# Norm sums of block 1 as two one-pass products of split squares, in a two-block transformer kernel on one core

## The chip, the core and the metric

The kernel runs on one core of a Trainium2 chip. The core has a matrix engine (TensorE, PE in the rows), a vector engine (VectorE, DVE), an activation engine (ScalarE, ACT), GpSimd (POOL) and a queue engine that issues the transfers (SP). Each takes its instructions in the order in which the program lists them and waits at an instruction until its semaphores have the value it asks for. The metric is the device time of one execution, in microseconds (us), the median of several. The engines share SBUF; products are written to PSUM, which has eight banks of 128 x 512 numbers.

## The reference

One sequence of 512 tokens, width 1024, float32. Block 1 (a parallel mixer: attention and a gated delta rule, both from one projection of the normed input) is what is changed; block 2 (stick-breaking attention, differential attention, two feed-forward layers) follows and is untouched. What matters of block 1:

```
q = apply_rope(rms_norm(heads(aq), q_norm)); k = apply_rope(rms_norm(heads(ak), k_norm))   # 8 and 2 heads
o_att = gqa_attention(q, k, v)
y_att = (o_att * silu(az)) @ w_br_att
qkv = silu(short_conv(concat([dq, dk, dv])))
qd = l2_norm(heads(cq)) * DN_DK ** -0.5 ; kd = l2_norm(heads(ck))                          # 8 and 8 heads
o_dn = bidir_gated_deltanet(qd, kd, vd, g, beta)
o_dn = rms_norm(o_dn, dn_norm)                                                             # 8 heads
y_dn = (o_dn * silu(dz)) @ w_br_dn
mix = (sigmoid(gate_att) * y_att + sigmoid(gate_dn) * y_dn) @ w_out
```

Both norms need, for each token, the sum of 128 squares of a head: 10 times for attention, 16 times for the convolved q and k, 8 times for the output.

## The kernel before

Everything is held feature-major: a tile is 128 features by 512 tokens. A sum over the features of a head is a product with a 128 x 128 matrix of ones, which also spreads the sum over all partitions.

**Projections.** Weights stream from memory in pairs of 1 MB, are split into a rounded high part (ACT, `w_hi`) and a rest (DVE, `w_lo`, line 2286), both in the type float32r, and each 128 x 128 block of weights gives three one-pass products of 512 columns (high by high, high by low, low by high). The high and low parts of the input lie in `hh` and `hl`, those of the weights in `spl`. Eight blocks, 24 products, make one output tile (a "projection"). They go to PSUM banks 0 and 1 in turn.

**Lanes.** All the rest of block 1 runs between these products. For each of 8 heads there are lanes: `rope_lane` (norm and rotation of attention's q), `att_lane`, `conv_lane` (five taps, SiLU, norm, for q, k and v), `prep_lane` (decay products, then a triangular inverse in levels of 32 x 32 products, `lv_m`, `lv_x`, ending in the 64 x 64 products `lv_q1` and `lv_q2`), `scan_lane` (four steps of `sc_r`, `sc_v`, `sc_s`, `sc_o`) and `out_lane` (the output norm: `on_a` squares it, `on_b` sums and applies it). A head's scan can begin once its `lv_q2` is through.

**The order** is set before the program runs, by `arrange`: it walks through the projections and keeps one clock per engine, adding a given cost for each step (0.86 us for a sum over features, `PE_B`; 0.69 for a DVE operation, 0.62 for an ACT operation). A lane's next step is put between two products when the lane's time and the engines it names are not ahead of PE's clock. Where the projections need something of a lane (`o.until`), the lane's steps are put down one after the other, with no product between them, until it is there. Such places are: a free pad before a convolution's projection; a free slot for the gated `dz` before its projection (`dz_slots`: the slot of head hd is given back by `on_b` of head hd - 2); a free bank; and, for the products of `w_br_att` (`ya`), each of its eight operands. These operands are reloaded from memory after `lv_q2` of head 7, split by ACT (`re_hi`) and DVE (`re_lo`, line 2529), and `ya` waits for the k-th before its k-th block.

**The sums** that are changed are plain float32 products: `ar_ss` (attention, its square in an `arena` tile), `cv_r` (convolution, its square in a `pad` or `x` tile), `on_b` (its square in `on_t`). In the rows a product is named by its output, its moving and its stationary operand: `ps<-pad,cst` is a square times the ones in `cst`; one plain product is two records there. In the scan `arena` alone (128x128) and `rv,arena` are `sc_v`, `rv,kdt` is `sc_s`, `arena,rv` is `sc_o`, `st,arena` is `sc_r`, `arena,st` the part of the state, `sc_oq`; in attention `x,arena` is the output (`at_o`), `cst,x` a transpose, `arena` with 512 columns the scores.

Of the kernel before, what the change touches and what calls it, by code (L numbers as in the profile page):

```python
# [234 lines left out]
def arrange(o, n_pairs):  # L235
# [161 lines left out]
    def rope_in(key, u):  # L397
# [4 lines left out]
        st = o.add("ar_in", key, cost=[("AC", AC_B), ("AC", AC_B)], after=u.t)  # L402
# [6 lines left out]
    def rope_lane(key, u):  # L409
# [136 lines left out]
    keep, work, acc, pads = Slots(2), Slots(1), Slots(2), Slots(4)  # L546
# [73 lines left out]
    def conv_lane(i, ip, t_in):  # L620
# [35 lines left out]
        st = o.add("cv_sq", i, cost=[("AC", AC_B)])  # L656
        st.ia, st.ip = ia, ip
# [7 lines left out]
        st = banked("cv_r", i, cost=[("PE", PE_B), ("AC", AC_B), ("AC", AC_B)])  # L665
        st.ip = ip
# [122 lines left out]
    def out_lane(hd, ikeep, ou):  # L789
        keep.give(ikeep, scan_last[hd])  # L790
        yield "AC"
        st = o.add("on_a", hd, cost=[("AC", AC_B), ("AC", AC_B)])
        st.u = ou
        obank.give(ou)
        yield "PE"
# [3 lines left out]
        st = banked("on_b", hd, cost=[("PE", PE_B), ("AC", AC_B), ("AC", AC_B), ("DV", DV_B), ("DV", DV_B)])  # L799
# [709 lines left out]
def build(nc, wstream, wba, consts, vecs, cossin, pos, xT, pT, outT):  # L1509
# [6 lines left out]
    with ctx:  # L1516
        def sb(name, shape, dt=F32):
            return ctx.enter_context(nc.sbuf_tensor(name, shape, dt))
# [39 lines left out]
        const_r = sb("const_r", [128, 320], F32R)  # L1558
        CR = {"neg_tri_l": const_r[:, 0:128]}
# [270 lines left out]
        def tensor(pe):  # L1830
# [9 lines left out]
            for q in steps:  # L1840
# [52 lines left out]
                elif kind == "ar_ss":  # L1893
# [3 lines left out]
                    w.wait_ge(*ar_in_done(q.key[0]))  # L1897
                    mm(psum[u.b][:, :], C["ones"], tmp_of.get(q.key[0], ar_tmp)[2], True, True).then_inc(filled[u.b], 1)
# [68 lines left out]
                elif kind == "cv_r":  # L1967
# [3 lines left out]
                    w.wait_ge(sem("cv_sq"), at["cv_sq", q.key[0]].n)  # L1971
                    mm(psum[u.b][:, :], C["ones"], pad_of[q.ip], True, True).then_inc(filled[u.b], 1)
# [149 lines left out]
                elif kind == "on_b":  # L2122
# [653 lines left out]
        def scalar(act):  # L2776
# [57 lines left out]
            for q in steps:  # L2834
# [589 lines left out]
```

## Time and profile before

| | us |
|---|---|
| runs | 2187.49, 2189.46, 2189.53; median 2189.46 |
| span of the profiled execution | 2186.7 |
| median over this span | 2.8 |
| busy in the span: PE, DVE, ACT, POOL | 2133.8, 1247.0, 1038.3, 224.2 |
| heads of block 1, 60 to 720 us: PE, DVE, ACT busy | 637.1, 424.5, 396.0 of 660 |

The profile gives one execution; its span is from its first to its last instruction, and the 2.8 us above it are the difference to the median of the timed runs. "Busy" of PE is the time in which some product is under way. Products overlap, so what one costs in a row of products is the step from its start to the start of the next, not its duration.

### The profile page before, as it was taken

How to read it: one execution, taken by the hardware profiler on the slowest of the kernel's cores; microseconds unless marked ns; L12 is line 12 of the kernel's file. 1: busy time of each engine (PE TensorE's matmuls, PEld its weight loads, DVE VectorE, ACT ScalarE, POOL GpSimd, SP SyncE). 2: the span in 40 equal slices, each digit the busy share in tenths (PEclk: the TensorE clock that was granted, in tenths of full speed). 3: DMA queues.
4: the chain of work that ended last, by engine and by line, in shares of the span. 5: the costliest groups of instructions: out<-in, count | busy, mean ns of one | idle time of the engine just before them, and what ended most of it. 6: DMA issues, size and time to landing. Idle time of an engine off the chain costs nothing.

```text
span 2186.7 us, 35850 instructions
## 1 busy us (share of the span) xinstructions
PE 2133.8 (98%) x14982; PEld 1685.9 (77%) x14982; DVE 1247.0 (57%) x2247; ACT 1038.3 (47%) x2012; POOL 224.2 (10%) x240
## 2 busy tenths in 40 slices
PE   8999999999999999999999999999999999999999
PEld 6777676777777887877777888888777777888887
DVE  6667677666654456655557542445577676443442
ACT  6656565566555235656655332233455544332331
POOL 0112221221220010100001000000101001000000
PEclk9999999999999999999999999999999999999999
DMA  4221211221214432211112222222211112222222
GB/s 177 99 79 63 78 65 50 89 68 50 97 50 153 142 135 78 70 67 59 58 39 82 97 97 97 97 97 97 82 62 63 63 59 97 97 97 96 97 97 77
DMA packets 36226, 186.68 MB, mean 85 GB/s; under 512 B 4560, under 2 KB 4944, under 8 KB 16992
## 3 DMA queue, kind: packets, MB, share of 16 engines
q1 hardware_dynamic: 36064, 184.38, 24.7%
q8 instruction: 118, 1.93, 0.4%
q14 instruction: 44, 0.36, 0.1%
HBM read 172.80 MB, written 7.90 MB: 83 GB/s over the span
## 4 chain that ended last, share of the span: by engine, by line
PE 89%; DVE 6%; ACT 3%; issue 2%; DMA 0%; SPq 0%; POOL 0%; DVEq 0%; ACTq 0%
PE ps L1834 88%; PE ps L1837 1%; ACT arena L2779 1%; DVE spl L2286 1%; ACT spl L2782 0%; ACT hh L2779 0%; DVE x L2644 0%; DMA raw<-wstream 0%; DVE x L2402 0%; DVE arena L2587 0%; DVE x L2573 0%; DVE arena L2485 0%; DVE arena L2569 0%; DVE hl L2595 0%; ACT on_t L2779 0%
## 5 line engine op out<-in xcount | busy, mean ns | idle before, releaser
L1834 PE MATMUL ps<-hh,spl 128*128 128x512 f32 (+1 forms) x3152 | 1024.1, 399 | 6.4 <-DVE hl L2577 2.1
L1834 PEld LDWEIGHTS ps<-hh,spl 128*128 128x128 f32 x3152 | 584.6, 189 | 139.5 <-issue 19.6
L1834 PE MATMUL ps<-hl,spl 128*128 128x512 f32 (+1 forms) x1568 | 620.8, 396 | 0.0
L2286 DVE TENSOR_TENSOR spl<-raw,spl 128x512 fp32r<-128x512 f32 x596 | 421.2, 731 | 153.6 <-ACT spl L2782 152.4
L1834 PE MATMUL ps<-arena_r,spl 128*128 128x512 f32 x1968 | 467.2, 392 | 10.3 <-DVE arena_r L2298 8.4
L1834 PEld LDWEIGHTS ps<-arena_r,spl 128*128 128x128 f32 x1968 | 371.1, 189 | 89.6 <-issue 10.5
L2782 ACT ACTIVATE spl<-raw 128x512 fp32r<-128x512 f32 x596 | 345.3, 619 | 143.9 <-PE ps L1834 138.8
L1834 PEld LDWEIGHTS ps<-hl,spl 128*128 128x128 f32 x1568 | 295.9, 189 | 63.0 <-issue 9.1
L1834 PE MATMUL ps<-arena 32*32 32x32 f32 (+6 forms) x5664 | 218.2, 224 | 16.8 <-issue 10.5
L2779 ACT ACTIVATE arena<-arena 128x512 f32<-128x512 f32 (+3 forms) x220 | 142.3, 648 | 189.7 <-DVE arena L2649 140.8
L1834 PEld LDWEIGHTS ps<-arena 32*32 32x32 f32 (+4 forms) x5664 | 126.2, 116 | 98.2 <-issue 79.4
L2782 ACT ACTIVATE arena_r<-arena 128x512 fp32r<-128x512 f32 x64 | 40.3, 631 | 197.0 <-DVE arena L2656 191.7
L2644 DVE TENSOR_TENSOR x<-x,ps 128x512 f32<-128x512 f32 x64 | 43.8, 684 | 133.6 <-PE ps L1834 133.6
L2779 ACT ACTIVATE arena<-ps 128x256 f32<-128x256 f32 (+5 forms) x116 | 69.0, 599 | 99.8 <-PE ps L1834 98.2
L2779 ACT ACTIVATE arena<-ps,small 128x512 f32<-128x512 f32 (+3 forms) x126 | 70.9, 566 | 90.0 <-DVE small L2745 53.9
L3248 POOL TENSOR_TENSOR arena<-arena 128x512 f32<-128x512 f32 x29 | 38.6, 1332 | 616.0 <-ACT arena L2779 616.0
L1834 PE MATMUL ps<-spl,hh 128*128 128x256 f32 x512 | 98.0, 291 | 2.7 <-DVE pad L2720 1.5
L2653 DVE TENSOR_TENSOR arena<-ps,arena 128x512 f32<-128x512 f32 x44 | 30.4, 691 | 104.4 <-PE ps L1834 104.4
L1834 PEld LDWEIGHTS ps<-spl,hh 128*128 128x128 f32 x512 | 80.8, 192 | 9.9 <-issue 6.2
L2649 DVE TENSOR_TENSOR arena<-ps,arena 128x512 f32<-128x512 f32 x44 | 30.4, 691 | 77.2 <-PE ps L1834 74.8
L1834 PE MATMUL ps<-spl,hl 128*128 128x256 f32 x256 | 72.6, 284 | 0.0
L2782 ACT ACTIVATE arena<-ps 128x256 f32<-128x256 f32 (+2 forms) x88 | 39.5, 449 | 65.0 <-PE ps L1834 51.2
(258 smaller groups left out, 2117.0 us busy)
## 6 DMA issues: line engine op xcount, KB each, us to landing
raw<-wstream SPq DMA_DIRECT2D x148, 1024.0 KB, 4.9
arena<-spill SPq DMA_DIRECT2D x17, 256.0 KB, 5.3
GS<-g_rows SPq DMA_DIRECT2D x16, 256.0 KB, 3.4
spill<-x SPq DMA_DIRECT2D x14, 256.0 KB, 2.0
arena<-arena SPq DMA_DIRECT2D x18, 128.0 KB, 2.2
x<-xT SPq DMA_DIRECT2D x4, 512.0 KB, 6.4
spill<-arena SPq DMA_DIRECT2D x8, 256.0 KB, 2.0
x<-xT SPq DMA_DIRECT2D x1, 2048.0 KB, 7.8
```

The costliest lines, as they stand in the source:

```text
L1834: return pe.matmul(out, lhsT, rhs, start=start, stop=stop, skip_group_check=True)
L1837: return pe.transpose(out, in_, C["ident"])
L2286: tt(spl[:, p % 2, 1, c], raw[:, p % 2, c], spl[:, p % 2, 0, c].bitcast(F32), ALU.subtract) \
L2644: tt(X[q.m], X[q.m], psum[q.u.b][:, :], ALU.add).then_inc(drained[q.u.b], 1)
L2649: tt(f_sl[q.i], psum[q.u.b][:, :], SQ[q.name][2], ALU.mult).then_inc(drained[q.u.b], 1)
L2653: tt(p, psum[q.u.b][:, :], SQ[q.g.name][2], ALU.mult).then_inc(drained[q.u.b], 1)
L2779: return act.activation(out, in_, func, **kw)
L2782: return act.activation(out, in_, ACT.Copy)
L3248: tt(acc, acc, tmp[q.i], ALU.add).then_inc(sem("sq_pool"), 1)
```

## The change

Each of the 34 sums becomes two one-pass products, of the high part of the square and of its rest, with ones in float32r (`ones_r`). For this, ACT writes the square a second time, rounded to float32r, and DVE subtracts the two (`ar_lo`, `cv_lo`, `on_lo`). Five tiles are added to the arena, the high part of the convolution has two slots (`sq_hi`), and the gates' semaphores are merged into one. The costs given to `arrange` change with it: 0.46 for a sum (`PE_S2`), an operation more on ACT and on DVE. Since `arrange` decides by these costs, the whole order of block 1 is another one. The last line of the diff makes room in SBUF.

```diff
+PE_S2 = 0.46
@@ rope_in, rope_lane
-        st = o.add("ar_in", key, cost=[("AC", AC_B), ("AC", AC_B)], after=u.t)
+        st = o.add("ar_in", key, cost=[("AC", AC_B)] * 3, after=u.t)
...
+        yield "DV"
+        o.add("ar_lo", key, cost=[("DV", DV_B)])
         yield "PE"
         while not ring.ready():
             yield "PE"
-        banked("ar_ss", key, cost=[("PE", PE_B), ("AC", AC_B), ("AC", AC_B)])
+        banked("ar_ss", key, cost=[("PE", PE_S2), ("AC", AC_B), ("AC", AC_B)])
@@ conv_lane
-        st = o.add("cv_sq", i, cost=[("AC", AC_B)])
-        st.ia, st.ip = ia, ip
+        while not sq_hi.ready():
+            yield "AC"
+        ih, h_old = sq_hi.take()
+        o.behind(h_old)
+        st = o.add("cv_sq", i, cost=[("AC", AC_B), ("AC", AC_B)])
+        st.ia, st.ip, st.ih, st.h_old = ia, ip, ih, h_old
+        yield "DV"
+        st = o.add("cv_lo", i, cost=[("DV", DV_B)])
+        st.ip, st.ih = ip, ih
...
-        st = banked("cv_r", i, cost=[("PE", PE_B), ("AC", AC_B), ("AC", AC_B)])
+        st = banked("cv_r", i, cost=[("PE", PE_S2), ("AC", AC_B), ("AC", AC_B)])
@@ out_lane
-        st = o.add("on_a", hd, cost=[("AC", AC_B), ("AC", AC_B)])
+        st = o.add("on_a", hd, cost=[("AC", AC_B)] * 3)
         st.u = ou
         obank.give(ou)
+        yield "DV"
+        o.add("on_lo", hd, cost=[("DV", DV_B)])
@@ tensor: cv_r (ar_ss and on_b alike)
-                    w.wait_ge(sem("cv_sq"), at["cv_sq", q.key[0]].n)
-                    mm(psum[u.b][:, :], C["ones"], pad_of[q.ip], True, True).then_inc(filled[u.b], 1)
+                    w.wait_ge(sem("cv_lo"), at["cv_lo", q.key[0]].n)
+                    mm(psum[u.b][:, :], ones_r[:, :], cv_hi[q.ih], True, False)
+                    mm(psum[u.b][:, :], ones_r[:, :], pad_lo[q.ip], False, True).then_inc(filled[u.b], 1)
@@ vector
+                elif kind == "cv_lo":
+                    w.wait_ge(sem("cv_sq"), at["cv_sq", q.key[0]].n)
+                    tt(pad_lo[q.ip], pad_of[q.ip], cv_hi[q.ih].bitcast(F32), ALU.subtract).then_inc(sem("cv_lo"), 1)
@@ scalar: on_a
+                    f(on_hi, psum[q.u.b][:, :], ACT.Square)
                     f(on_e, psum[q.u.b][:, :], ACT.Square)
                     f(on_o, psum[q.u.b][:, :], ACT.Identity, scale=V("dn_norm")).then_inc(drained[q.u.b], 1)
@@
-    nc = _bacc.Bacc("TRN2", target_bir_lowering=False, num_devices=1)
+    nc = _bacc.Bacc("TRN2", target_bir_lowering=False, num_devices=1, dynamic_dma_scratch_size=1024)
```

**The first place that moves: PE, the scan of head 5.** Before, projection products (`hh,spl`, `hl,spl`) stand between its steps; from `lv_q2` (64x64) on:

```order
L1834 MATMUL ps<-arena 64x64 x8
L1834 MATMUL ps<-hl,spl 128x512
L1834 MATMUL ps<-x,arena 128x128 x4
L1837 MATMUL ps<-cst,x 128x128 x4
L1834 MATMUL ps<-arena 128x512
L1834 MATMUL ps<-arena 128x128 x2
L1834 MATMUL ps<-hh,spl 128x512 x2
L1834 MATMUL ps<-hl,spl 128x512
L1834 MATMUL ps<-hh,spl 128x512
L1834 MATMUL ps<-rv,kdt 128x128 x2
L1834 MATMUL ps<-arena,rv 128x128 x2
L1834 MATMUL ps<-hh,spl 128x512
```

Now it stands between the projections of head 6's `dz` and head 7's `dz`; from `lv_q2` (64x64) on:

```order
L1857 MATMUL ps<-arena 64x64 x8
L1857 MATMUL ps<-arena 128x128 x2
L1857 MATMUL ps<-rv,kdt 128x128 x2
L1857 MATMUL ps<-arena,rv 128x128 x2
L1857 MATMUL ps<-st,arena 128x128 x2
L1857 MATMUL ps<-rv,arena 128x128 x2
L1857 MATMUL ps<-arena,st 128x128 x2
L1857 MATMUL ps<-x,arena 128x128 x4
L1860 MATMUL ps<-cst,x 128x128 x4
L1857 MATMUL ps<-arena 128x512
L1857 MATMUL ps<-rv,kdt 128x128 x2
L1857 MATMUL ps<-arena,rv 128x128 x2
```

and it ends with `on_b`, the pair with `on_r`, before the first product of head 7's `dz`:

```order
L1857 MATMUL ps<-arena,rv 128x128 x2
L1857 MATMUL ps<-st,arena 128x128 x2
L1857 MATMUL ps<-rv,arena 128x128 x2
L1857 MATMUL ps<-arena,st 128x128 x2
L1857 MATMUL ps<-arena,rv 128x128 x2
L1857 MATMUL ps<-arena_r,ones_r 128x512
L1857 MATMUL ps<-on_r,ones_r 128x512
L1857 MATMUL ps<-hh,spl 128x512
L1857 MATMUL ps<-hl,spl 128x512
```

What moved: the 32 rows from `lv_q1` to `on_b` of this head hold no projection product, where before there were 48 between `lv_q1` and `on_b`. `on_b` of head 5 stands behind 1416 projection products, before behind 1269. Two shorter stretches of this sort are new as well: five half-levels of 32x32 products with one product of scores between them (behind product 1200), and two and two with one sum between them (behind 1512).

**The second place: PE and DVE at the end of head 7.** Before, its scan and `on_b` were over 42 products ahead of `ya` (the row of 576, whose moving operand is `arena_r`):

```order
L1834 MATMUL ps<-arena,rv 128x128 x2
L1834 MATMUL ps<-hh,spl 128x512
L1834 MATMUL ps<-hl,spl 128x512
L1834 MATMUL ps<-hh,spl 128x512 x2
L1834 MATMUL ps<-hl,spl 128x512
L1834 MATMUL ps<-hh,spl 128x512
L1834 MATMUL ps<-on_t,cst 128x512
L1834 MATMUL ps<-hh,spl 128x512
L1834 MATMUL ps<-hl,spl 128x512
L1834 MATMUL ps<-hh,spl 128x512 x2
L1834 MATMUL ps<-hl,spl 128x512
```

Now `ya` begins within the scan, and `on_b` stands between the blocks 3 and 4 of its first tile:

```order
L1857 MATMUL ps<-arena,rv 128x128 x2
L1857 MATMUL ps<-arena_r,spl 128x512 x2
L1857 MATMUL ps<-st,arena 128x128 x2
L1857 MATMUL ps<-arena_r,spl 128x512 x2
L1857 MATMUL ps<-rv,arena 128x128 x2
L1857 MATMUL ps<-arena,st 128x128 x2
L1857 MATMUL ps<-arena_r,spl 128x512 x2
L1857 MATMUL ps<-arena,rv 128x128 x2
L1857 MATMUL ps<-arena_r,spl 128x512 x3
L1857 MATMUL ps<-arena_r,ones_r 128x512
L1857 MATMUL ps<-on_r,ones_r 128x512
L1857 MATMUL ps<-arena_r,spl 128x512 x564
```

On DVE, `re_lo` of the eight operands (2529, now 2566) stood before like this around the two steps of `on_b` (2515 and 2518, now 2552 and 2555):

```order
L2529 TENSOR_TENSOR arena_r<-arena,arena_r 128x512
L2508 SCALAR_TENSOR_TENSOR st<-st,small,ps 128x128 x2
L2529 TENSOR_TENSOR arena_r<-arena,arena_r 128x512
L2495 SCALAR_TENSOR_TENSOR rv<-ps,small,arena 128x128 x2
L2529 TENSOR_TENSOR arena_r<-arena,arena_r 128x512 x2
L2515 TENSOR_TENSOR arena<-arena,on_t 128x512
L2518 TENSOR_TENSOR arena<-arena 128x512
L2286 TENSOR_TENSOR spl<-raw,spl 128x512
L2529 TENSOR_TENSOR arena_r<-arena,arena_r 128x512
```

and now:

```order
L2566 TENSOR_TENSOR arena_r<-arena,arena_r 128x512
L2545 SCALAR_TENSOR_TENSOR st<-st,small,ps 128x128 x2
L2532 SCALAR_TENSOR_TENSOR rv<-ps,small,arena 128x128 x2
L2566 TENSOR_TENSOR arena_r<-arena,arena_r 128x512 x2
L2313 TENSOR_TENSOR spl<-raw,spl 128x512
L2363 TENSOR_TENSOR on_r<-on_t,arena_r 128x512
L2552 TENSOR_TENSOR arena<-arena,on_t 128x512
L2555 TENSOR_TENSOR arena<-arena 128x512
L2566 TENSOR_TENSOR arena_r<-arena,arena_r 128x512 x3
L2313 TENSOR_TENSOR spl<-raw,spl 128x512
L2566 TENSOR_TENSOR arena_r<-arena,arena_r 128x512
```

What moved: `on_b` of head 7 stands behind 1692 projection products, before behind 1638; `ya` begins behind 1680 in both. The operands 4 to 6 of `ya` are split behind both steps of `on_b` on DVE, and PE asks for operand 4 right behind the sum of `on_b`.

## Rows read from the trace of the kernel before

**Rows 1.** Busy time by stretch: PE, PEld, DVE, ACT, POOL, clock, DMA share, GB/s.

```profile
60.00:720.00 660.00, 637.10 (x7820) 493.06 (x7819) 424.50 (x858) 396.03 (x795) 133.54 (x144) 0.99 0.23 79
```

**Rows 2.** PE's waits, 60 to 720 us: us in total, times, longest.

```profile
PE ps L1834 <- issue: 10.5, 11, 3.2
PE ps L1834 <- DVE arena L2485: 4.6, 7, 1.2
```

**Rows 3.** PE in order of time: start, us; a sum and its neighbours.

```profile
69.74 1.02 PE L1834 MATMUL ps<-pad,cst 128*128 128x512 f32 x2
...
70.83 0.40 PE L1834 MATMUL ps<-hl,spl 128*128 128x512 f32 x1
71.06 0.62 PE L1834 MATMUL ps<-hh,spl 128*128 128x512 f32 x2
```

**Rows 4.** Groups by line, 60 to 720 us: busy us, mean ns, idle before.

```profile
L2286 DVE TENSOR_TENSOR spl<-raw,spl 128x512 fp32r<-128x512 f32 x132 | 97.2, 751 | 28.2 <-ACT spl L2782 27.8
...
L2779 ACT ACTIVATE pad<-x 128x512 f32<-128x512 f32 x12 | 7.5, 627 | 5.0 <-DVE x L2407 3.8 <-DVE x L2402 1.3
```

**Rows 5.** PE in order of time: lv_q2 and on_b of heads 2, 3, 7.

```profile
315.71 0.68 PE L1834 MATMUL ps<-arena 64*64 64x64 f32 x16
...
342.04 1.02 PE L1834 MATMUL ps<-on_t,cst 128*128 128x512 f32 x2
...
380.39 0.68 PE L1834 MATMUL ps<-arena 64*64 64x64 f32 x16
...
403.48 1.10 PE L1834 MATMUL ps<-on_t,cst 128*128 128x512 f32 x2 [0.67 <-ACT arena L2779]
...
668.60 0.68 PE L1834 MATMUL ps<-arena 64*64 64x64 f32 x16
...
686.91 1.10 PE L1834 MATMUL ps<-on_t,cst 128*128 128x512 f32 x2
```

**Rows 6.** PE in order of time: pieces of attention, then of the scan.

```profile
516.93 1.05 PE L1834 MATMUL ps<-x,arena 128*128 128x128 f32 x8
517.82 0.60 PE L1837 MATMUL ps<-cst,x 128*128 128x128 f32 x4
518.26 1.02 PE L1834 MATMUL ps<-arena 128*128 128x512 f32 x2
...
671.72 0.67 PE L1834 MATMUL ps<-rv,kdt 128*128 128x128 f32 x4
...
672.59 0.48 PE L1834 MATMUL ps<-hl,spl 128*128 128x512 f32 x1
```

**Rows 7.** PE, ACT and DVE in order of time: two half-levels of head 7.

```profile
656.07 0.75 PE L1834 MATMUL ps<-arena 32*32 32x32 f32 x64
...
656.87 0.38 ACT L2782 ACTIVATE arena<-ps 128x256 f32<-128x256 f32 x1 [2.87 <-PE ps L1834]
...
659.41 0.42 DVE L2457 TENSOR_TENSOR arena<-arena,ps 128x256 f32<-128x256 f32 x1 [3.35 <-PE ps L1834]
659.87 0.45 DVE L2459 STREAM_TRANSPOSE arena<-arena 128x256 f32<-128x256 f32 x1
```

**Rows 8.** ACT and DVE in order of time: behind on_b of head 7.

```profile
688.04 0.69 ACT L2779 ACTIVATE on_t<-ps,small 128x512 f32<-128x512 f32 x1 [0.28 <-PE ps L1834]
...
689.43 0.69 DVE L2515 TENSOR_TENSOR arena<-arena,on_t 128x512 f32<-128x512 f32 x1 [3.40 <-ACT on_t L2779]
690.16 0.69 DVE L2518 TENSOR_TENSOR arena<-arena 128x512 f32<-128x512 f32 x1
```

**Rows 9.** PE in order of time, then stretches as in rows 1.

```profile
227.00 0.43 PE L1834 MATMUL ps<-arena 32*32 32x32 f32 x16 [3.22 <-issue]
...
222.00:224.00 2.00, 1.78 (x62) 1.18 (x53) 0.18 (x1) 0.90 (x2) 1.82 (x3) 1.00 0.95 383
...
225.00:230.00 5.00, 3.00 (x22) 2.12 (x21) 2.10 (x4) 0.60 (x1) 0.00 (x0) 0.64 0.01 3
230.00:235.00 5.00, 5.00 (x140) 3.92 (x140) 0.48 (x2) 2.10 (x5) 0.00 (x0) 0.68 0.00 0
```

More of the change, by code:

```diff
@@ L664, in conv_lane @@
             o.behind(o.at["pr_kk", hd - 1])
-        st = banked("cv_r", i, cost=[("PE", PE_B), ("AC", AC_B), ("AC", AC_B)])
-        st.ip = ip
+        st = banked("cv_r", i, cost=[("PE", PE_S2), ("AC", AC_B), ("AC", AC_B)])
+        st.ip, st.ih = ip, ih
+        sq_hi.give(ih, st)
         yield "DV"
@@ L798, in out_lane @@
         o.behind(o.at["dz_out", hd])
-        st = banked("on_b", hd, cost=[("PE", PE_B), ("AC", AC_B), ("AC", AC_B), ("DV", DV_B), ("DV", DV_B)])
+        st = banked("on_b", hd, cost=[("PE", PE_S2), ("AC", AC_B), ("AC", AC_B), ("DV", DV_B), ("DV", DV_B)])
         dz_slots.give(hd % 2, st)
@@ L1531, in build @@
         spl = sb("spl", [128, 2, 2, 2048], F32R)
-        x = sb("x", [128, KT, S])
+        with nc.sbuf_tensor("x", [128, KT, S], F32) as x:
+            pass
+        x_r = sb("x_r", [128, KT, S], F32R)
         hh = sb("hh", [128, KT, S], F32R)
         hl = sb("hl", [128, KT, S], F32R)
-        NA = 41
+        NA = 46
         with nc.sbuf_tensor("arena", [128, NA, S], F32) as arena:
@@ L1558, in build @@
         const_r = sb("const_r", [128, 320], F32R)
+        ones_r = sb("ones_r", [128, 128], F32R)
         CR = {"neg_tri_l": const_r[:, 0:128]}
@@ L1896, in tensor @@
                         w.wait_ge(drained[u.b], u.n - 1)
-                    w.wait_ge(*ar_in_done(q.key[0]))
-                    mm(psum[u.b][:, :], C["ones"], tmp_of.get(q.key[0], ar_tmp)[2], True, True).then_inc(filled[u.b], 1)
+                    w.wait_ge(sem("ar_lo"), at["ar_lo", q.key[0]].n)
+                    hi, lo = ar_halves(q.key[0])
+                    mm(psum[u.b][:, :], ones_r[:, :], hi, True, False)
+                    mm(psum[u.b][:, :], ones_r[:, :], lo, False, True).then_inc(filled[u.b], 1)
                 elif kind == "gate_mm":
@@ L2125, in tensor @@
                         w.wait_ge(drained[u.b], u.n - 1)
-                    t = at["on_a", hd].u
-                    w.wait_ge(drained[t.b], t.n)
-                    mm(psum[u.b][:, :], C["ones"], on_e, True, True).then_inc(filled[u.b], 1)
+                    w.wait_ge(sem("on_lo"), hd + 1)
+                    mm(psum[u.b][:, :], ones_r[:, :], on_hi, True, False)
+                    mm(psum[u.b][:, :], ones_r[:, :], on_lo, False, True).then_inc(filled[u.b], 1)
                 elif kind == "rstd" and q.last:
@@ L2275, in vector @@
             dve.tensor_copy(ident_r[:, :], C["ident"]).then_inc(sem("setup"), 1)
+            dve.tensor_copy(ones_r[:, :], C["ones"])
             dve.memset(eps, EPS).then_inc(sem("setup"), 1)
@@ L2881, in scalar @@
                     f(rs, k_in[i], ACT.Square)
+                    f(ar_halves(q.key[0])[0], k_in[i], ACT.Square)
                     f(t_, k_in[i], ACT.Identity, scale=V("k_norm")).then_inc(sem("ar_in"), 1)
@@ L2891, in scalar @@
                     f(rs, psum[q.u.b][:, :], ACT.Square)
+                    f(ar_halves(name)[0], psum[q.u.b][:, :], ACT.Square)
                     f(t_, psum[q.u.b][:, :], ACT.Identity, scale=qw).then_inc(drained[q.u.b], 1)
@@ L2898, in scalar @@
                     full(u)
-                    f(g3(beta), db, ACT.Exp, scale=-1.0).then_inc(sem("gate_eb"), 1)
+                    f(g3(beta), db, ACT.Exp, scale=-1.0).then_inc(sem("gate_act"), 1)
                     empty(u)
@@ L2948, in scalar @@
                     w.wait_ge(sem("cv_act"), at["cv_act", q.key[0]].n)
+                    if q.h_old:
+                        full(q.h_old.u)
+                    f(cv_hi[q.ih], acc_of[q.ia], ACT.Square)
                     f(pad_of[q.ip], acc_of[q.ia], ACT.Square).then_inc(sem("cv_sq"), 1)
```

31 lines of the change are left out of this document (21 added, 10 removed).

## The prediction

> **What bounds the kernel now.** I read the busy times first: over the heads of block 1, 60 to 720 us, PE is busy 637.1 of 660 us, DVE 424.5 (64%), ACT 396.0 (60%) [rows 1]. So PE is the bound, at close to full clock. Next come PE's waits: the largest is "issue", 10.5 us in 11 gaps, that is, gaps in which no semaphore was awaited; the second is the product behind `lv_q2`, 4.6 us in 7 [rows 2]. No wait on the ends of the norm sums is among the large ones. So a shorter product is time won as long as PE stays fed; what decides is whether the new order keeps it fed.
>
> **What is removed: three eighths of a sum each, on the path.** A plain sum starts at 69.74; the projection product behind the next one starts at 70.83, and the one after it 0.23 us later [rows 3]. So the sum and one projection product take 1.09 us, the sum alone 0.86. The pair is two one-pass products, 0.46 us. That is 0.40 us less for each of 34 sums: **-13.6 us**. The rows of a projection are the nearest ones for a pair, since they too change their weights at each product, so I give this term no more than 1 us either way.
>
> A page of the Trainium skill, "TensorE: Matmul & The Clock Gate" (section "Back-to-back issue gap"), gives a gap of N/2.4 ns plus 2.5 ns for one pass, 216 ns at 512 columns. By it the pair would be 0.43 us and the term -14.6 us. The row shows 0.23 us for one product in this kernel, and the row decides.
>
> **What is added on ACT and DVE, off the path.** 34 squares on ACT at 0.63 us, like the group with 128x512 in and out, and 34 subtractions on DVE at 0.75 us at most, like the one with the same shape and types [rows 4]: 21 and 26 us, by which ACT goes from 60% to 63% and DVE from 64% to 68%. Neither becomes the bound. In a chain that ends in a sum they come one behind the other and lengthen it by 0.6 + 0.7 = 1.3 us, which costs nothing while projection products stand between. They cost where none do.
>
> **What is moved: block 1's order.** The lanes come later against the projections: `on_b` of head 5 behind 1416 products, not 1269; of head 7 behind 1692, not 1638. Late lanes cost nothing by themselves. They cost at the places where the planner had to have something finished, and there put the steps of a chain one behind the other. Nothing of that sort stood in the order before. The places, one by one:
>
> *Head 5's scan, behind product 1416.* PE has to go through all rows from `lv_q1` to `on_b` before the next projection product. How long the chain takes is read from the same chain before: from `lv_q2` to `on_b` 26.3 us (head 2), 23.1 us (head 3), 18.3 us (head 7, with no attention beside it) [rows 5]. Part of the longer ones is the filling itself, so I take 22.3 us, add 1.3 us for the new square and subtraction, and 3 us from `lv_q1` to `lv_q2`, between which a piece of each kind of attention stands: 26.6 us. PE's own work in it: 17 pieces of the scan at 0.44 (7.4 us), four outputs of attention at 0.89, three transposes at 0.44 [rows 6], two scores at 0.86 like a sum, two 64x64 pieces at some 0.4 (an estimate), one pair: 15.3 us. Left over are 11 us; I book **+10**. The ends: with head 7's chain 7 us, with head 2's 15 us.
>
> *The levels, behind 1200 and 1512.* From a level's products to ACT 0.80 us, ACT 0.38; from the other half to DVE as long, and DVE 0.42 and 0.45 [rows 7]. So a half-level takes 1.2 and 1.7 us in turn, of which PE works 0.7. Five in a row with one product of scores: 5.9 - 4 x 0.7 - 0.86 = 2.2 us idle. Two pairs with a sum between: some 2 us. On top, such bursts run short of instructions: the ten "issue" gaps beside the largest come to 0.7 us each (10.5 less 3.2, over 10) [rows 2]; one or two more of them in nine dense bursts: 1 us. Together **+5**, ends 3 and 9. A further scan step without filling behind product 1104: **+1**.
>
> Here too a page speaks: "Runtime: NRT & Kernel Launch" of the Trainium skill, section "Instruction fetch mechanics", holds that fetching is hidden behind the pace of issue. This trace disagrees: PE stood still for 3.22 us within a burst, with nothing awaited, just as a load of weights moved 383 GB/s [rows 9]. By the page the places would be 1 us cheaper.
>
> *The end of head 7, behind 1680.* Now only 28 projection products are there to fill the scan and its `on_b`, not 34, and the chain is 1.3 us longer: 6 x 0.23 + 1.3 = 2.7 us. Then comes a new wait: PE asks for operand 4 of `ya` right behind the sum of `on_b`, and on DVE its `re_lo` stands behind both steps of `on_b`, which wait for ACT. Before, `on_b`'s sum began at 686.91 [rows 5], ACT took it up at 688.04, DVE at 689.43 and 690.16 [rows 8], so the split of operand 4 would end near 690.85 + 0.7 = 691.5. The pair begins at 687 and takes 0.46, so PE waits from 687.4 to 691.5: 4.1 us. Together **+7**, ends 4 and 9.
>
> **What goes with the old order.** The gap of 3.22 us, and what followed it: the granted clock was 0.64 and 0.68 in the 10 us from 225 to 235 us [rows 9], where half speed is 1.2 GHz; that is 3.4 us lost. A gap of this sort needs a burst just when weights land, and there are as many of both as before, so I count half of 6.6: **-3.3** (ends -6.6 and 0). Waits at head 5's old place, some **-1**.
>
> **The clock.** The new stretches have two idle times of 3 us and more: before `on_b` of head 5 (the last scan step, three ACT steps and the subtraction with nothing to fill), and before operand 4 of `ya`. Before the clock fell at 225 us, PE had idled for 3.22 us. One of the two will do it again: **+3.3**, ends 0 and 6.6.
>
> **The sum.** -13.6 + 10 + 5 + 1 + 7 - 3.3 - 1 + 3.3 = +8.4 us on a span of 2186.7: 2195.1. The median lies 2.8 us above that span: **2197.9 us**, against 2189.5.
>
> **The rivals.**
> 1. *The stretches are cheap* and the products' gain stays: all chains at their light end and no fall of the clock. -13.6 + 7 + 3 + 1 + 4 - 6.6 - 1 + 0 = -6.2 us, so 2183 us. For it: head 7's chain of 18.3 us shows what the scan needs without attention. Against it: attention is in the stretch of head 5, on the same ACT and DVE.
> 2. *They cancel.* Gain and new waits meet at 2185 to 2194 us, most simply when the clock doesn't fall and the luck of the old gap isn't repeated (8.4 - 3.3 - 3.3 = +1.8, so 2191 us).
> 3. *Instructions and clock.* The dense bursts run dry as at 223.8 us, and both idle times pull the clock down: 15 + 9 + 1 + 9 + 6.6 - 13.6 - 1 = +26 us, 2216 us. For it the gap of 3.22 us in a single burst, against it that the other ten gaps are short.
> 4. *The queues.* The added 21 and 26 us make ACT and DVE late in the dense stretches, so that ordinary steps arrive late at PE as well: 34 times 0.4 us is 14 us, which would eat the whole gain even if the stretches cost half: 2200 us. It decides from a DVE near 80%; the 64% of [rows 1] with the added work, 68%, speaks against it.
> 5. *The pair isn't cheaper*, if the new type slowed the plain products beside it: 0 instead of -13.6, 2211 us. Projection products of this type already stand beside plain ones [rows 3].
>
> **How the numbers follow.** The forecast (2194 to 2206 us) has 0.42; rival 1 0.19, rival 2 0.24, rival 3 0.06, rival 4 0.07, rival 5 0.02. A range of 8 in 10 has to take in rivals 2 and 4 and most of 1: 2182 to 2209 us. A measurement of this kernel can tell some 0.2% from no change, 4.4 us: faster is under 2185.1, slower over 2193.8. Faster 0.20, same 0.24, slower 0.56.
>
> **What would show it.** Right: PE's busy time down by some 14 us of products, `ps<-..,ones_r` at a step of 0.23 us; PE idle by some 10 us within the 27 us before `on_b` of head 5; a wait of PE for DVE line 2566 of some 4 us right behind head 7's `on_b`; waits in the bursts behind product 1200; a granted clock under 0.9 behind one of them. Wrong: if the stretch of head 5 lasts under 22 us, if PE's waits in block 1 grow by less than 10 us in all, or if they are spread over all heads and not at these places.

## The result: 20 us slower, and the profile after

| | before | changed |
|---|---|---|
| median, us | 2188.72 (2187.49 to 2189.53, 4 runs) | 2208.88 (2206.39 to 2210.47, 4 runs) |
| span of the profiled execution, us | 2186.7 | 2208.7 |
| PE busy in the span, us | 2133.8 | 2132.1 |
| mean granted clock of TensorE | 0.997 | 0.991 |

The ratio is 1.0096, with an interval of 1.0084 to 1.0109, or 21.0 us; by the medians it is 20.2 us more. The forecast was slower, by 8.4 us. Its direction held, its size didn't: the cost is more than twice what was booked, and the time lies at the very end of the range. Where the sum broke can be read from two lines of the table above. The span grew by 22.0 us, PE's busy time fell by 1.7, so PE idles 23.7 us more. The forecast had some 20 us more of idle time (10 + 5 + 1 + 7 - 1, less half of the old 3.2 us gap). That is 3.3 us too little. But PE's busy time should have fallen by 12.0 us (the 13.6 of the pairs, less the 3.3 of a new fall of the clock, plus 1.7 for half of the old one), and fell by 1.7: it is 11.9 us more than the pairs alone would have left. So 10.3 of the 13.6 us that were missed are there.

The first view is the stretch of [rows 1], of the changed kernel: us, busy us of PE, of the weight loads, DVE, ACT, POOL, then granted clock, DMA share and GB/s.

```profile
60.00:720.00 660.00, 616.51 (x7748) 484.54 (x7747) 431.08 (x874) 403.99 (x813) 128.97 (x144) 0.98 0.22 73
```

PE is busy 20.6 us less than in [rows 1], and 72 product records fewer lie in that time. Its waits in the same stretch, as in [rows 2] (us in total, times, longest):

```profile
PE ps L1857 <- DVE arena L2522: 7.1, 8, 1.5
PE ps L1857 <- issue: 5.4, 8, 1.7
PE ps L1857 <- DVE on_r L2363: 5.4, 4, 3.7
PE ps L1857 <- DVE arena_r L2566: 5.1, 3, 3.5
PE ps L1857 <- ACT x L2816: 4.7, 2, 3.4
PE ps L1857 <- ACT arena L2819: 4.7, 4, 2.0
```

"issue" fell from 10.5 to 5.4 us. New are the waits for the subtraction ahead of `on_b` (L2363), for the split operands of `ya` (L2566), for a projection's bank (ACT `x`) and for the levels (ACT `arena`). The long ones stand where the order has no projection products. PE in order of time, a sum of the changed kernel with its neighbours, and then the stretch of head 5's scan, from the last projection product ahead of it to the first behind it:

```profile
67.67 0.62 PE L1857 MATMUL ps<-arena_r,ones_r 128*128 128x512 f32 x2
68.13 0.40 PE L1857 MATMUL ps<-hl,spl 128*128 128x512 f32 x1
...
555.08 0.40 PE L1857 MATMUL ps<-hh,spl 128*128 128x512 f32 x1
556.82 0.68 PE L1857 MATMUL ps<-arena 64*64 64x64 f32 x16 [1.35 <-DVE arena L2515]
...
583.67 0.76 PE L1857 MATMUL ps<-arena_r,ones_r 128*128 128x512 f32 x1 [3.72 <-DVE on_r L2363]
584.24 0.63 PE L1857 MATMUL ps<-on_r,ones_r 128*128 128x512 f32 x1
584.66 0.63 PE L1857 MATMUL ps<-hh,spl 128*128 128x512 f32 x1
```

A pair takes 68.13 - 67.67 = 0.46 us, where a plain sum took 0.86 [rows 3]. Behind the last pair shown, the next product starts after 0.42 us, not 0.23: the engine is at half clock. Stretches of the changed kernel, with the columns of the first view; each but the first lies in or right behind a place without projection products:

```profile
50.00:55.00 5.00, 5.00 (x17) 3.88 (x16) 3.96 (x16) 3.56 (x9) 0.00 (x0) 0.68 0.40 165
460.00:465.00 5.00, 3.40 (x173) 1.99 (x174) 2.84 (x7) 1.05 (x3) 1.89 (x3) 0.72 0.02 3
580.00:585.00 5.00, 1.33 (x3) 1.16 (x4) 3.46 (x4) 2.91 (x6) 2.42 (x3) 0.73 0.11 38
585.00:590.00 5.00, 5.00 (x15) 3.87 (x14) 3.68 (x8) 3.24 (x6) 0.60 (x1) 0.59 0.22 64
625.00:630.00 5.00, 1.57 (x49) 1.02 (x49) 2.44 (x7) 2.25 (x5) 0.00 (x0) 0.66 0.02 3
630.00:635.00 5.00, 5.00 (x69) 3.64 (x59) 2.09 (x7) 1.95 (x4) 0.00 (x0) 0.50 0.00 0
635.00:640.00 5.00, 4.47 (x42) 2.83 (x40) 1.17 (x3) 0.87 (x2) 0.00 (x0) 0.81 0.61 213
715.00:720.00 5.00, 2.57 (x6) 2.08 (x7) 3.79 (x6) 1.89 (x4) 0.00 (x0) 0.54 0.35 111
720.00:725.00 5.00, 5.00 (x18) 3.55 (x18) 2.82 (x5) 2.93 (x5) 0.00 (x0) 0.78 0.34 99
```

In block 1 the clock fell five times, where it fell once before [rows 9]; in block 2 it falls three times in either kernel (at 1165, 1555 and 1580 us before, at 1185, 1575 and 1600 us in the changed one). What the clock lacks of 1.00 in these rows, times 5 us each, is 15.0 us; in the two rows of before it is 3.4. The difference, 11.6 us, is close to the 11.9 us that PE's busy time had too much, but partly by chance: during some of that time PE idled, and a slow clock costs an idle engine nothing. Multiplied by PE's busy time instead, the rows give 11.1 against 2.7 us, and slices of half a us, which part busy from idle better, 12.3 against 3.1. So the clock cost some 9 us more than before; I can't place the other 3 us of the 11.9. The Trainium skill describes this pattern in "TensorE: Matmul & The Clock Gate", section "HAM oscillation — how this bites in real kernels": a kernel whose PE waits between bursts pays twice, for the wait and for the half clock behind it. These rows agree (a wait of 3.72 us, then products at a step of 0.42 us and not 0.23), and the run with fillers below shows it directly.

### The profile page after: what moved, and what is told of

It reads as the page before. It is cut to its first block, busy times and chain, and to the rows that moved or that the text cites. A ratio compares the mean times of both kernels' runs of the same rounds, so it can differ in the third digit from the quotient of the medians.

```text
span 2208.7 us, 35927 instructions
## 1 busy us (share of the span) xinstructions
PE 2132.1 (97%) x14982; PEld 1691.8 (77%) x14982; DVE 1265.3 (57%) x2282; ACT 1055.1 (48%) x2046; POOL 219.9 (10%) x240
## 4 chain that ended last, share of the span: by engine, by line
PE 85%; DVE 8%; ACT 4%; issue 2%; DMA 1%; SPq 0%; POOL 0%; DVEq 0%; ACTq 0%
PE ps L1857 84%; DVE spl L2313 1%; PE ps L1860 1%; ACT arena L2816 1%; ACT spl L2819 1%; DMA on_t<-spill 1%; DVE arena L2439 0%; ACT hh L2816 0%; DVE x L2681 0%; ACT x L2816 0%; ACT arena L2819 0%; DMA raw<-wstream 0%; DVE x L2439 0%; DVE arena L2522 0%; DVE arena L2624 0%
## 5 line engine op out<-in xcount | busy, mean ns | idle before, releaser
L1857 PEld LDWEIGHTS ps<-hh,spl 128*128 128x128 f32 x3152 | 587.2, 189 | 143.0 <-issue 13.6
L1857 PE MATMUL ps<-arena_r,spl 128*128 128x512 f32 x1968 | 472.0, 394 | 18.0 <-DVE arena_r L2325 9.4
L1857 PE MATMUL ps<-arena 32*32 32x32 f32 (+6 forms) x5664 | 219.1, 225 | 20.3 <-DVE arena L2522 7.1
L3291 POOL TENSOR_TENSOR arena<-arena 128x512 f32<-128x512 f32 x29 | 38.7, 1334 | 613.9 <-ACT arena L2816 613.9
```

Of the source, the lines that this page charges most:

```text
L1857: return pe.matmul(out, lhsT, rhs, start=start, stop=stop, skip_group_check=True)
L3291: tt(acc, acc, tmp[q.i], ALU.add).then_inc(sem("sq_pool"), 1)
```

## Experiments

The theory after the result: (A) the new order costs, by idle PE and by the clock that falls behind it; the pairs give their 13.6 us, and the added squares and subtractions are nearly free. The first rival (B): these cost, wherever they stand.

### The three orders, with the old and the new work

`e1_old_order`: the changed kernel's work in the order of before. The planner gets the costs of before, so that it puts down the same steps in the same order, and each subtraction is put on DVE where its square is done, by a pass behind it:

```diff
-        yield "DV"
-        st = o.add("cv_lo", i, cost=[("DV", DV_B)])
+        st = o.low("cv_lo", i, st, ("cv_r", i))
...
-        st = banked("cv_r", i, cost=[("PE", PE_S2), ("AC", AC_B), ("AC", AC_B)])
+        st = banked("cv_r", i, cost=[("PE", PE_B), ("AC", AC_B), ("AC", AC_B)])
```

> The sums are split as in the changed kernel (pair of one-pass products, second square on ACT, subtraction on DVE), but every other step of every engine stands in the order of the kernel before; each subtraction stands on DVE where its square is just done. Theory A (the new order costs, the split itself pays): the 34 pairs give back 13.6 us and the 0.6 + 0.7 us on ACT and DVE are covered, so 2175 us, between 2172 and 2179. Rival B (the added work on ACT and DVE makes PE wait wherever it stands): 2188 us or more. Rival C (the pair is no cheaper than a plain sum on PE): 2189 us, with PE's busy time as before.

Measured: 2216.80 us, ratio 1.0135 (1.012 to 1.015). The theory failed here, by 42 us, and rival B holds in this order. PE's waits, 60 to 720 us:

```profile
PE ps L1873 <- DVE arena_r L2373: 10.7, 6, 2.5
PE ps L1873 <- DVE pad_r L2376: 9.8, 7, 3.8
PE ps L1873 <- DVE on_r L2379: 5.1, 5, 1.9
...
PE ps L1873 <- DVE x_r L2376: 3.1, 5, 1.1
```

These are the subtractions: 28.7 us in 23 waits, at 34 sums. In the old order nothing leaves room for them: PE comes to the sum soon after the plain square, and now something of 0.7 us that queues on DVE stands between. PE's busy time doesn't fall here either (2133.7 us in the span), since the clock falls at more places (the mean is 0.992 to 0.993, against 0.996 to 0.999 before). This is the price of one way to put 34 subtractions into an order that wasn't made for them, and no bound for others.

`e2_old_order_plain`: the same, with one plain product for a sum.

```diff
-                    mm(psum[u.b][:, :], ones_r[:, :], cv_hi[q.ih], True, False)
-                    mm(psum[u.b][:, :], ones_r[:, :], pad_lo[q.ip], False, True)
+                    mm(psum[u.b][:, :], C["ones"], cv_hi[q.ih].bitcast(F32), True, True)
```

> As the run with the old order, all added ACT and DVE work kept, but each sum is one plain float32 product again, of the rounded square; the rest of the square is left out of the sum. Theory A: the added work is covered, so the kernel before plus 0 to 3 us, 2189 to 2192, and 13 to 14 us above the run with the pairs. Rival B: 2200 us or more. Rival C: the same time as the run with the pairs.

Measured: 2226.39 us, 1.0177 (1.016 to 1.0194). Rival B again; rival C falls, since the pairs are worth 0.42%, 9 us, even where PE waits at many of the sums (the intervals of the two ratios leave this figure open by some 5 us).

`e3_new_order_old_work`: the order of the changed kernel (its `arrange` untouched), the work of before. The steps of the subtractions issue nothing:

```diff
                 elif kind == "cv_lo":
-                    tt(pad_lo[q.ip], pad_of[q.ip], cv_hi[q.ih].bitcast(F32), ALU.subtract)
+                    pass
-                    f(cv_hi[q.ih], acc_of[q.ia], ACT.Square)
```

> The order of the changed kernel, but without its work: plain float32 sums, one square on ACT, no subtraction on DVE. Theory A (the order costs): the 20.3 us of the change plus the 13.6 us that the pairs had hidden, less up to 4 us since the chains in the stretches without projection products are shorter: 2219 to 2223 us. Rival B (the added work costs, not the order): 2195 us or less.

Measured: 2207.81 us, 1.0093 (1.0078 to 1.0108). The order alone costs 20.3 us, without any of the new work. (The kernel also keeps the changed one's added tiles, merged semaphores and scratch size; that these cost nothing is shown by `e5_slack_old_work` below, which has them too and isn't slower than the kernel before.) Both expectations missed: rival B falls for this order, but A had 2219 or more, since it took the added work as free. Then the new work as a whole (pairs and all) is worth nothing in this order, though the pairs should save PE 13.6 us.

`e10_new_order_plain`: the changed kernel with one plain product for a sum (the edit of `e2_old_order_plain`), which parts the two.

> The order and all added ACT and DVE work of the changed kernel, but each sum is one plain float32 product, of the rounded square; the rest is left out of the sum. With the run of the same order without the added work (0.9 to 1.0% above the kernel before) and the changed kernel it parts the price of the work from the gain of the pairs. Theory A (pairs give their 0.40 us wherever PE is not waiting at the sum, the work costs where a chain ends in a sum with nothing beside it): 8 to 11 us above the changed kernel, 2217 to 2220 us, so the added work costs 9 to 12 us in this order. Rival I (pairs give nothing in this order): within 3 us of the changed kernel.

Measured: 2220.82 us, 1.0158 (1.014 to 1.0175). As A had it, a little larger: the pairs give 0.62% or 13.6 us, and the added work costs 0.65% or 14.2 us. Each is a difference of two ratios and is known to some 5 us: that the first agrees with the booked 13.6 to the digit is luck (the medians give 11.9).

`e4_slack`, `e5_slack_old_work` and `e12_slack_plain` are the same three in a third order, which comes from one number of the planner:

```diff
-SLACK = 1.0
+SLACK = 1.5
```

> The changed kernel with one number of the planner changed: SLACK, by how far an engine named by a lane may be ahead of PE's clock when the lane's next step is put down, is 1.5 us and not 1.0. In the order that results, no run of lane steps without projection products is longer than 4 us by the planner's costs, where the changed kernel has one of 28 us, one of 9 and one of 6. Theory A: the cost of the order goes and the pairs' 13.6 us stay, but waits of 1 to 2.6 us remain at some ten places: 2172 to 2184 us. Rival B: 2205 us or more, since the work is the same.

> The order of the run with SLACK at 1.5 us, with the old work: plain float32 sums, one square on ACT, no subtraction on DVE. Theory A (in an order with products between the steps the pair is worth its full price, and the added work is covered): 34 times 0.40 = 13.6 us above the 2176.5 of that run, 2186 to 2191 us, about the kernel before. Theory D (the gain of 12 us came from a luckier order, and pairs and added work cancel as they did in the changed kernel's order, 2208.9 against 2207.8): within 3 us of 2176.5.

> The order and all added work of the run with SLACK 1.5, but each sum is one plain float32 product of the rounded square, the rest left out. Theory A (pairs are worth 13.6 us here less what waits take back; the rest of the gap to the run with the old work, 7 us, is the added work): 10 to 13 us above the 2176.5 of that run, 2187 to 2190 us, that is 3 to 6 us above the run with the old work. Rival K (the added work is free here and the pairs are worth only 7 us): 2182 to 2184 us, as with the old work.

Measured: 2176.55 us, 0.9951 (0.9933 to 0.9969); 2182.20 us, 0.9984 (0.9975 to 0.9993); 2186.61 us, 1.0005 (0.9996 to 1.0014). The first is 12 us faster than the kernel before and 32 us faster than the changed kernel, with the same work. The second lies between the two expectations: the new work as a whole is worth 7 us, not 13.6. The third says why: pairs 11.8 us (10 to 13 expected), added work 4.6 us (3 to 6 expected), as A had it, though each is known to no better than 3 to 4 us.

`e11_before_slack`: is 1.5 simply the better number?

> The kernel before with SLACK 1.5 us instead of 1.0 and nothing else. Theory A (the constant suits one set of costs; the kernel before had a good order already): no gain, 2187 to 2195 us. Rival J (1.5 us is simply the better constant, and the split has no part in the gain of the run with SLACK 1.5): 2175 to 2180 us.

Measured: 2187.55 us, 1.0007 (0.9998 to 1.0016). No: with the costs of before, 1.0 is as good. Other numbers were not tried on the kernel before. Together, as ratios to the kernel before, and the steps between them in us (2187 times the difference):

| order | old work | + squares, subtractions | + pairs | added work | pairs |
|---|---|---|---|---|---|
| of before | 1 | 1.0177 | 1.0135 | +38.7 | -9.2 |
| of the changed kernel | 1.0093 | 1.0158 | 1.0096 | +14.2 | -13.6 |
| with SLACK 1.5 | 0.9984 | 1.0005 | 0.9951 | +4.6 | -11.8 |

Each of these steps is uncertain by 3 to 5 us, from the intervals of its two ratios. So the pairs' column agrees with the forecast, and its three values can't be told apart. The added work's can: what was booked as nearly free costs between 5 and 39 us, by what stands around it. The time of the third order's rows, 60 to 720 us with the columns of the first view: PE is busy 23 us more than in the changed kernel, at a clock that rounds to 1.00.

```profile
60.00:720.00 660.00, 639.51 (x7876) 502.36 (x7875) 451.47 (x897) 414.04 (x834) 135.05 (x144) 1.00 0.24 83
```

### What the added work does at a chain's end

Compare the end of head 5's scan with the new and with the old work, in the same order. First the changed kernel, ACT and DVE, then the run with the old work, ACT and PE:

```profile
579.72 3.20 DVE L2439 SCALAR_TENSOR_TENSOR arena<-x,vec,arena 128x511 f32<-128x511 f32 x3
...
579.99 0.60 ACT L2816 ACTIVATE arena_r<-ps 128x512 fp32r<-128x512 f32 x1 [0.28 <-PE ps L1857]
580.49 0.59 ACT L2816 ACTIVATE on_t<-ps 128x512 f32<-128x512 f32 x1
580.97 0.69 ACT L2816 ACTIVATE arena<-ps,vec 128x512 f32<-128x512 f32 x1
582.84 0.68 DVE L2363 TENSOR_TENSOR on_r<-on_t,arena_r 128x512 fp32r<-128x512 f32 x1
```

```profile
586.46 0.60 ACT L2809 ACTIVATE on_t<-ps 128x512 f32<-128x512 f32 x1 [0.28 <-PE ps L1857]
586.95 0.68 ACT L2809 ACTIVATE arena<-ps,vec 128x512 f32<-128x512 f32 x1
587.77 0.67 PE L1857 MATMUL ps<-on_t,cst 128*128 128x512 f32 x1 [1.36 <-ACT arena L2809]
```

PE waits 1.36 us with the old work and 3.72 with the new: the second square is 0.5 of it, the subtraction 0.7, and 1.2 us it stood behind three convolution taps that DVE had in its queue since 579.72. And the clock: 552 to 600 us, the changed kernel and then the run with the old work.

```profile
552.00:600.00 48.00, 38.11 (x282) 31.15 (x283) 28.93 (x62) 28.90 (x57) 8.92 (x10) 0.93 0.13 45
```

```profile
552.00:600.00 48.00, 41.05 (x380) 31.51 (x379) 27.50 (x63) 30.54 (x62) 8.75 (x10) 1.00 0.14 45
```

Behind the wait of 1.36 us the clock stays up; with that of 3.72 us it is at half from 582.3 to 589.1 us, of which PE is busy 5.4 us. That costs 2.7 us on top of the 2.4. The rest is read from the run with plain sums, `e10_new_order_plain`, against the run with the old work: 0.8 us ahead of the first sum, some 2 us on the way to product 1416, and more at the levels of head 6. The two profiled executions differ by 10.0 us only, not by 14.2, so a part lies between executions: over all four, the mean clock is 0.990 with the added work and 0.9945 without. I can't put a place to each part.

### The clock by itself

`e6_fill`: products that nobody needs, while PE waits.

```diff
+            def fill(u, n):
+                for _ in range(n):
+                    mm(psum[u.b][:, :], ones_r[:, :], HI["hh"][0], True, True)
...
+                    fill(u, 14 if hd == 5 else 0)
                     w.wait_ge(sem("on_lo"), hd + 1)
```

and the same in the levels, as the expectation lists them.

> The changed kernel, with fillers: one-pass products of 512 columns into the bank of the step that follows, overwritten by it, while PE waits for that step's data. 14 before the sum of on_b of head 5 (wait of 3.72 us), 8, 2 and 4 in the levels of head 4 behind product 1200 (waits of 2.00, 0.59 and 1.00 us), 5 and 3 in those of head 6 behind product 1512 (1.37 and 0.71 us). They shorten no wait. Theory A (a fall of the clock behind an idle PE is a cost of its own): the clock stays at full speed behind the two first places, where it was half for some 5 and 3 us, which gives back 2.6 + 1.4 = 4 us, and up to 2 more at the third: 2203 to 2206 us. Rival E (the clock falls for another reason than the idle PE, so busy products don't hold it): 2208 to 2210 us, granted clock under 0.8 at 580 to 590 us as before.

Measured: 2201.41 us, 1.0076 (1.0058 to 1.0095), 4.4 us under the changed kernel by the ratios. Its stretches around the two first places, and the third:

```profile
575.00:580.00 5.00, 4.03 (x23) 3.35 (x23) 4.85 (x10) 3.16 (x7) 1.89 (x2) 1.00 0.37 105
580.00:585.00 5.00, 4.61 (x21) 3.44 (x20) 2.72 (x5) 3.77 (x7) 1.45 (x2) 1.00 0.00 0
585.00:590.00 5.00, 5.00 (x26) 4.10 (x25) 3.44 (x9) 2.99 (x7) 0.29 (x1) 1.00 0.66 216
625.00:630.00 5.00, 5.00 (x87) 3.49 (x88) 1.06 (x4) 1.95 (x4) 0.00 (x0) 0.50 0.01 3
...
460.00:465.00 5.00, 4.82 (x144) 3.44 (x143) 2.65 (x7) 1.74 (x5) 1.90 (x3) 1.00 0.02 5
```

At full clock where the changed kernel had 0.72, 0.73 and 0.59; at the third place, whose last wait of 3.3 us has no bank free for fillers, it still fell (0.50). The intervals of the two ratios overlap, so what makes it sure is the trace. Head 5's scan, from `lv_q1` through the 14 fillers to the next pair behind the stretch, in the run with fillers, and the last of these rows of the changed kernel:

```profile
554.79 0.68 PE L1857 MATMUL ps<-arena 64*64 64x64 f32 x16 [1.35 <-DVE arena L2522]
...
577.68 3.52 PE L1857 MATMUL ps<-hh,ones_r 128*128 128x512 f32 x14
581.58 0.50 PE L1857 MATMUL ps<-arena_r,ones_r 128*128 128x512 f32 x1 [0.39 <-DVE on_r L2370]
...
589.26 0.39 PE L1857 MATMUL ps<-arena_r,ones_r 128*128 128x512 f32 x1
```

```profile
593.82 0.39 PE L1857 MATMUL ps<-arena_r,ones_r 128*128 128x512 f32 x1
```

The chain was not shortened: from the start of the last scan step (577.21 us, and 579.25 in the changed kernel) to the sum it is 4.37 us, against 4.42. But from `lv_q1` to the next pair it takes 34.5 us with fillers and 37.0 without (593.82 - 556.82). These 2.5 us are the clock's alone, and the expectation had 2.6 for this place. The levels of head 4 gave 0.8 us by the same reckoning, where it had 1.4. The rest of the gap between the two profiled executions (2199.1 against 2208.7 us) has other sources: one is a fall of the clock at 50 us, which the run with fillers was spared though nothing was changed there. In its four executions the time goes with the clock too: three at a mean clock of 0.995 took 2201.0 to 2201.8 us, one at 0.991 took 2207.8.

### The places

`e7_operands_first`: `on_b` of head 7, and the first reload of the operands of the other output product (`yd`), behind the split of `ya`'s operand 6.

```diff
+    st = order.at["on_b", 7]
+    order.steps.remove(st)
+    behind = order.at["re_lo", "ya", 6]
+    for k in (order.at["re_ld", "yd", 0],):
+        order.steps.remove(k)
+    i = order.steps.index(behind) + 1
+    order.steps[i:i] = [st, order.at["re_ld", "yd", 0]]
```

> The changed kernel, with on_b of head 7 (its sum, its two ACT steps and its two DVE steps) and the first reload of yd's operands put behind the split of ya's operand 6, nothing else moved. Theory A (PE's 3.5 us wait for re_lo of operand 4 is only its place behind both DVE steps of on_b): that wait goes, 1 to 2 us of waiting for the reload of operands 6 and 7 takes its place, and PE's clock stays up at 715 to 725 us (2 us): 2204 to 2207 us. Rival F (the operands come late because of their reloads, whatever stands ahead of them): 2208 to 2210 us.

Measured: 2210.31 us, 1.0105 (1.0086 to 1.0123), no gain that shows above the width of the intervals. PE at the same place:

```profile
719.16 2.76 PE L1864 MATMUL ps<-arena_r,spl 128*128 128x512 f32 x6 [1.71 <-DVE arena_r L2573]
721.72 0.63 PE L1864 MATMUL ps<-arena_r,ones_r 128*128 128x512 f32 x1
722.15 0.63 PE L1864 MATMUL ps<-on_r,ones_r 128*128 128x512 f32 x1
722.57 0.98 PE L1864 MATMUL ps<-arena_r,spl 128*128 128x512 f32 x3
726.87 1.65 PE L1864 MATMUL ps<-arena_r,spl 128*128 128x512 f32 x3 [3.32 <-DVE arena_r L2573]
```

The wait of 3.50 us moved from operand 4 to operand 7 (3.32 us), which now stood behind `on_b`'s steps on ACT and DVE, and one of 1.71 us came ahead of it. The 1.71 us are within the 1 to 2 us that theory A had for the reloads of the operands 6 and 7; the 3.32 us neither expectation had. The place was right, the remedy wasn't: in both orders the operand that stands behind `on_b` is late.

`e9_late_slot`: the last `dz` projection takes its slot only when its SiLU begins, so that nothing forces head 5's scan through.

```diff
...
+        if i is None:
+            while dz_slots.held[1]:
+                yield
+            i, old = dz_slots.take()
...
         if hd == 7:
-            o.until(lambda: not dz_slots.held[1])
             gemm(h, KT, z_done("dz", 7, dz_slots))
```

> The changed kernel, where the last projection of dz no longer waits for a free slot before its products: its SiLU takes the slot, and the projection's bank waits. So PE need not go through head 5's scan without projection products at product 1416. Theory A (that stretch costs some 10 us of idle PE and 2.6 us of clock by itself): 2198 to 2201 us if nothing takes its place. Rival H (the lanes' backlog is the cause, and a stretch only the place where it is worked off): by the planner's costs a stretch of 17 us in head 6's levels and scan and one of 8 us take its place, and it is 2204 to 2209 us.

Measured: 2199.98 us, 1.0061 (1.0046 to 1.0076), 7.7 us under the changed kernel: within the 2198 to 2201 us that A had for a stretch that simply goes. But the trace shows rival H's mechanism. Some of its stretches:

```profile
585.00:590.00 5.00, 2.40 (x11) 2.02 (x10) 0.69 (x1) 3.97 (x8) 2.69 (x3) 0.76 0.23 52
615.00:620.00 5.00, 2.52 (x139) 2.20 (x143) 2.36 (x6) 0.65 (x2) 0.00 (x0) 0.50 0.01 3
620.00:625.00 5.00, 1.45 (x80) 1.21 (x75) 1.79 (x8) 3.33 (x8) 0.00 (x0) 0.50 0.02 3
625.00:630.00 5.00, 2.93 (x35) 2.56 (x36) 2.78 (x6) 1.42 (x3) 0.00 (x0) 0.50 0.00 0
630.00:635.00 5.00, 4.20 (x17) 3.32 (x16) 1.18 (x4) 1.94 (x4) 1.18 (x2) 0.50 0.02 3
```

Head 6's levels and scan are now the stretch without projection products, at half clock for over 20 us. What had fallen behind is worked off at the next place that asks for it. The 7.7 us are what is left between two stretches; what head 5's cost in full, this run can't say, since another took its place.

`e8_margin`: a search over two of the planner's numbers, by its own costs.

```diff
-SLACK = 1.0
-MARGIN_1 = 0.0
+SLACK = 1.8
+MARGIN_1 = -0.15
```

> The changed kernel with two numbers of the planner changed: SLACK 1.8 us, and block 1's margin -0.15 us (a lane's step may be put down when its data is due within 0.15 us, not only when it is due). By the planner's costs PE idles 14.9 us in block 1, against 24.6 with SLACK 1.5 and 53.6 in the changed kernel. Theory A (what PE waits by the planner's costs is what decides): some 6 to 10 us under the 2176.5 of the run with SLACK 1.5, 2166 to 2172 us. Rival G (the planner's clock is too coarse for the last 10 us): 2174 to 2182 us.

Measured: 2175.01 us, 0.9949 (0.9934 to 0.9964), the lowest time of all, but its ratio can't be told from that of `e4_slack`. Rival G holds: the planner's costs tell an order with a stretch of 28 us from one without, but not two good orders that differ by 10 us on its own clock.

## Why the prediction was right and wrong, step by step

- **The pairs, -13.6 us: right.** 0.46 against 0.86 us in the rows. In whole kernels they gave 13.6, 9.2 and 11.8 us in the three orders, each to some 5 us, so the runs confirm the size and no more.
- **The order: right in sum, in part by luck.** Without the 1.3 us for the new work in two chains, the forecast for the order was 22 - 2.6 = 19.4 us, and the order alone costs 20.3. But of the 19.4, 17.8 were idle time and 1.6 the clock. In the profiled execution of `e3_new_order_old_work` PE idles 14.8 us more than before and is busy 6.4 us more, with the same products. So the idle time was put 3 us too high and the clock some 5 us too low.
- **The places were right.** Head 5's scan: from `lv_q1` to the sum it lasts 583.67 - 556.82 = 26.9 us against the 26.6 worked out. From 555.4 to 584.6 us PE is busy 19.3 of 29.2 us, 9.9 idle against the 10 booked, though 1.35 us of it stand ahead of `lv_q1`, where nothing was booked. The end of head 7: 1.07 + 0.54 + 1.11 + 3.50 us of waits, 6.2 against 7, with 3.50 us for operand 4 where 4.1 was worked out. The levels were too small: 3.6 us behind product 1200 and 6.6 behind 1512, together 10.2, against 5 with the instruction supply (whose sum has 5.9 us for four steps of 1.2 and 1.7 in turn, which make 5.8). At the second, the last wait of 3.37 us is for the bank of the next projection (ACT `x`), which I had not put at that place.
- **The clock, wrong: the step that failed.** I took the two idle times of 3 us and more, gave one of them a fall (+3.3 us), and counted half of the old order's fall as gone (half of 3.4), so the clock came to +1.6 us net. It fell five times in block 1, also behind a row of shorter waits (2.00, 0.59 and 1.00 us at 456 to 465 us), and cost some 9 us more than before. I had drawn a rule from the one gap of [rows 9], as if it took an idle time of that length. The old fall went wholly, and by PE's busy time the five new ones cost 12.3 us, where 3.3 were booked. (I had also counted 3.4 us for the old fall though PE idled for a part of it; by PE's busy time it was 3.1.)
- **The added ACT and DVE work, wrong in this order too.** "Costs nothing while projection products stand between" holds only where the sum's place has moved behind it, and "1.3 us" at a chain's end left out the queue: 2.4 us at head 5, of which 1.2 us behind three taps. I booked 2.6 us, and the runs show 14.2 (to some 5 us), in part by the clock again. The two failures are largely the same microseconds counted along two lines: by idle time and clock, or by order and work.
- **Waits of the old order** went further than said: "issue" fell by 5.1 us, where half of the 3.2 us gap was booked as gone and 1 us as new in the bursts.
- **Rivals.** Number 3 had the right mechanism in its half on the clock, though instruction supply had little part in it: "issue" is lower than before, and the longest such gap is 1.7 us. Number 4 (the queues) named the price that showed, 14 us, but not its cause, so its figure is luck: it wanted DVE near 80%, and 65% (431.08 of 660 us) was enough where a subtraction meets three taps.

## To carry to other kernels

Where a planner sets an order from a table of costs, a change of the costs is a change of the order, and the kernel before stands at a number that suits its own costs (here 1.0 and 1.5 gave it the same time). Look for the number again before the change is judged: here that was worth 32 us, and turned +20 us into -12. Work on an engine at 65% is not free if PE asks for it at once: count the queue ahead of it, at each chain that ends in it. Count a stretch in which PE waits long or often twice, once for the idle time and once for the half clock behind it (at head 5, 3.7 us and 2.7 us). If the stretch can't be avoided, products without use in its bank can keep the clock, as 14 of them did here.

## What the runs showed of the hardware

The granted clock also fell behind three shorter waits in a row (2.00, 0.59 and 1.00 us, at 456 to 465 us), and stayed up behind a wait of 1.36 us at the end of head 5's scan with the old work. The falls aren't the same in each execution of one order. The changed kernel fell at 49.6 us, behind a single wait of 1.31 us, and the run with fillers, with the same order and work there, stayed up behind its wait of 1.30 us. `e7_operands_first`, which is the changed kernel up to head 7, fell to 0.50 at some 566 us as well, within head 5's scan, behind waits of 1.35 and 1.54 us and in one of 0.71 us; the changed kernel stayed up behind the same waits. So the length of one wait doesn't decide alone.

The time goes with the clock: the run with fillers has mean clocks of 0.995, 0.995, 0.995 and 0.991 and a spread of 7 us over its four executions, the changed kernel 4 us, and `e8_margin` 0.4 us at a clock of 0.998 each time. But few falls don't promise a small spread: the kernel before, at 0.996 to 0.999, lies between 2183.6 and 2190.4 us.
